# A fused encoder layer: tile 0's own queries among the attention pieces of tiles 1 to 3, paired forgetting scores, a fifth late query head

## The reference, cut to what matters

```
xn = rmsnorm(x); qa,ka,va,fa,qb,kb,vb = split(xn @ w_in)
A: 8 heads of 64: softmax(qa ka^T/8 + c_q - c_k, causal) va,   c = cumsum(log_sigmoid(fa + b_f))
B: 4 heads of 128: (softmax(q1 k1^T/8 + alibi) - lam softmax(q2 k2^T/8 + alibi)) vb, block-causal, rmsnorm
h  = x + [A || B] @ w_out
hn = rmsnorm(h); q = hn @ w_q                       # 8 retrieval heads, two halves of 128
s1,i1 = top16(q1 keys1^T); s2,i2 = top16(q2 keys2^T)
top16 of s1+s2 -> 16 experts e of 16384, gate g = softmax
h += sum_k gelu(u[e_k] . hn) g_k v[e_k];            out = rmsnorm_final(h)
```

## Time and profile before

| | us |
|---|---|
| median of the runs | 1546.19 |
| profiled execution, its own time | 1543.74 |
| its span, first to last instruction | 1542.0 |
| TensorE busy | 1278.2 (83%) |
| VectorE busy | 1078.2 (70%) |
| GpSimd busy | 757.8 (49%) |
| ScalarE busy | 459.6 (30%) |
| DMA moved | 596.5 MB, mean 387 GB/s |

### The profile page before, as it was taken

The page is one execution under the profiler, slowest core; times in us unless marked ns, Lnnn a source line. Parts: engine busy times, 40 slices in busy tenths (PEclk is TensorE's granted clock), DMA queues, the critical chain, the costliest instruction groups (busy, mean ns, idle before and its releaser), DMA issues.

```text
span 1542.0 us, 13063 instructions
## 1 busy us (share of the span) xinstructions
PE 1278.2 (83%) x3727; PEld 661.2 (43%) x3727; DVE 1078.2 (70%) x2520; ACT 459.6 (30%) x1200; POOL 757.8 (49%) x637
## 2 busy tenths in 40 slices
PE   9999999988888298999776788777787788777777
PEld 8776655665545144444332333332333333333333
DVE  3257699999988776666666676666666776666654
ACT  3432355466233032222222222221222222222212
POOL 0027477775677444454544544444455454444550
PEclk9999999998989599999999998899999999998999
DMA  9669799997999999999999999999999999999995
GB/s 381 260 248 414 277 324 347 374 376 262 350 362 392 400 391 407 423 421 421 422 421 422 421 422 421 421 422 421 421 421 422 422 421 422 422 421 421 421 421 215
DMA packets 99741, 596.50 MB, mean 387 GB/s; under 512 B 11480, under 2 KB 11480, under 8 KB 42328
## 3 DMA queue, kind: packets, MB, share of 16 engines
q0 software_dynamic: 89856, 536.91, 86.1%
q1 hardware_dynamic: 9816, 58.77, 9.5%
HBM read 593.54 MB, written 2.10 MB: 386 GB/s over the span
## 4 chain that ended last, share of the span: by engine, by line
DMA 43%; PE 15%; DVE 6%; POOL 2%; ACT 2%; issue 2%; DVEq 0%; POOLq 0%
PE acc L993 13%; DMA map_mem<-in_peer_uv_dram,eidx 9%; DMA w_ring<-in_peer_uv_dram,eidx 7%; DMA v_all<-in_peer_uv_dram,eidx 7%; DMA act_mem<-in_peer_uv_dram,eidx 6%; DMA mix_mem<-in_peer_uv_dram,eidx 5%; DMA v_ring<-in_peer_uv_dram,eidx 4%; DMA u_ring<-in_peer_uv_dram,eidx 4%; DMA v_ring<-in_peer_v_dram,eidx 2%; PE mm L785 1%; ACT diag L1226 1%; DVE map_mem L1544 1%; DVE w_ring L1544 1%; PE sc L785 1%; POOL v_ring L691 1%
## 5 line engine op out<-in xcount | busy, mean ns | idle before, releaser
L1219 ACT ACTIVATE gel<-hid 128x4 f32<-128x4 f32 x126 | 25.8, 205 | 713.7 <-DVE hid L1544 704.6
L684 POOL DMA_INDIRECT u_ring<-in_peer_u_dram,eidx x112 | 139.7, 1247 | 171.5 <-DVE eidx L1524 98.6
L993 PE MATMUL acc<-v_all,diag 128*128 128x512 f32 x256 | 128.3, 647 | 65.5 <-ACT diag L1226 65.0
L691 POOL DMA_INDIRECT v_ring<-in_peer_v_dram,eidx x112 | 132.3, 1182 | 64.0 <-DVE h L1572 35.4
L1572 DVE SCALAR_TENSOR_TENSOR h<-v_ring,coef,h 128x1024 f32<-128x1024 f32 x112 | 143.9, 1285 | 16.2 <-DMA v_ring<-in_peer_v_dram,eidx 13.0
L1536 DVE CUSTOM_DVE_ANT_0 u_ring<-u_ring,hn 128x1024 f32<-128x1024 f32 x112 | 136.4, 1218 | 14.0 <-DMA u_ring<-in_peer_u_dram,eidx 13.8
L993 PE MATMUL acc<-v_ring,diag 128*128 128x512 f32 x248 | 123.6, 645 | 27.2 <-ACT diag L1226 23.6
L993 PE MATMUL acc<-u_ring,diag 128*128 128x512 f32 x248 | 123.5, 645 | 26.1 <-ACT diag L1226 24.5
L993 PE MATMUL acc<-map_mem,diag 128*128 128x512 f32 x248 | 120.7, 633 | 25.3 <-ACT diag L1226 25.3
L1226 ACT ACTIVATE diag<-ident,coef 128x128 f32<-128x128 f32 x392 | 126.2, 390 | 48.2 <-DVE coef L1562 39.6
L710 POOL DMA_INDIRECT v_all<-in_peer_uv_dram,eidx x64 | 81.0, 1265 | 89.3 <-PE acc L993 81.4
(11 more groups left out here) (281 smaller groups left out, 2335.9 us busy)
## 6 DMA issues: line engine op xcount, KB each, us to landing
w_ring<-in_slabs_dram SPq DMA_DIRECT2D x29, 1024.0 KB, 8.3
v_ring<-in_slabs_dram SPq DMA_DIRECT2D x6, 1024.0 KB, 11.0
u_ring<-in_slabs_dram SPq DMA_DIRECT2D x6, 1024.0 KB, 11.4
map_mem<-in_slabs_dram SPq DMA_DIRECT2D x6, 1024.0 KB, 8.5
h<-in_x_dram SPq DMA_DIRECT2D x4, 512.0 KB, 13.1
u_ring<-in_peer_u_dram,eidx POOLq DMA_INDIRECT x112, 6.6
v_ring<-in_peer_v_dram,eidx POOLq DMA_INDIRECT x112, 6.9
v_all<-in_x_cols_dram SPq DMA_DIRECT2D x3, 512.0 KB, 7.3
```

Source lines behind the costliest of these rows:

```text
L684: nc.gpsimd.indirect_dma_start(out=u_ring[:, c % U_RING, :], out_offset=None, in_=peer_u[0], in_offset=bass.IndirectOffsetOnAxis(ap=eidx[n ...
L691: nc.gpsimd.indirect_dma_start(out=v_ring[:, c % V_RING, :], out_offset=None, in_=peer_v[0], in_offset=bass.IndirectOffsetOnAxis(ap=eidx[n ...
L993: last = nc.tensor.matmul(acc[half][:, :], diag[:, c % COLS, :], v_row(n, c)[:, half * BANK:(half + 1) * BANK], start=first, stop=(n % PH ...
L1219: nc.scalar.activation(gel[:, par, g0:g0 + COLS], hid[:, par, g0:g0 + COLS], ACT.Gelu).then_inc(gelu_done, 1)
```

## The change

It has four parts.

1. Order. Tile 0's remaining queries and keys (heads 3 to 7) no longer stand ahead of tiles 1 to 3, but among their pieces, head by head. For this tile 0's `hT` is kept in the memory of `gfb` (`h0T`), its query rows in a buffer of their own (`own_q`), and SP loads `gfb` after all slabs but the last two, once tile 0's last query is done.
2. The gates of tiles 1 to 3. "forget" (TensorE's product) comes before the last query/key slab of mixer A; "gate" (VectorE up to the absolute value, ScalarE's Exp and Ln) and "decay" (VectorE's cumulative sum) are pieces of their own. They cost 6 and 0 in the plan.
3. Scores of mixer A are made in pairs of heads at even steps: both products on 64 rows, then both on 40.
4. Five late heads instead of four. And ScalarE's GELU comes at gap 0 instead of gap 4.

```
-LATE_HEADS = 4
+LATE_HEADS = 5
+        gates = [("forget", g)] if g == 0 else [("gate", g), ("decay", g)]
+        ps += fox_in[:values_at] + gates + fox_in[values_at:values_at + 1] + [("selq", g, tiles[0])] + fox_in[values_at + 1:]
+        if g > 0:
+            ps.insert(ps.index(("project", g, 3, 0)), ("forget", g))
...
-    BEFORE, later = first_pieces[:cut_at], first_pieces[cut_at:] + pieces_of(1)
+    BEFORE, own, later = first_pieces[:cut_at], first_pieces[cut_at:], []
+    total, at = sum(share(p) for p in own + pieces_of(1)), 0.0
+    heads = [[p for p in own if p[0] == "query" and p[2] // 2 == hd] + [("keys", 0, hd)] for hd in range(EARLY_HEADS, PH)]
+    due = [(GRP * (i + 1) - 2) / (SLOTS - 1) for i in range(len(heads))]
+    for p in pieces_of(1):
+        if heads and not heads[0]:
+            heads.pop(0)
+            due.pop(0)
+        if heads and at / total >= due[0]:
+            later.append(heads[0].pop(0))
+            at += share(later[-1])
+        later.append(p)
+        at += share(p)
...
+        h0T = gfb[:, :].rearrange("p (c n) -> p c n", c=KC)
+        own_q = sb("own_q", [P, SLAB])
...
-            sp.dma_start(gfb[:, :], final_g.rearrange("(a n) -> a n", a=1).broadcast_to([P, D])).then_inc(out_done, 16)
             for n in range(N_IN + N_OUT + 2, len(slab_order) - 2):
                 load_slab(n)
+            sp.wait_ge(mm_full, mm_done(("query", 0, 2 * PH - 2)))
+            sp.dma_start(gfb[:, :], final_g.rearrange("(a n) -> a n", a=1).broadcast_to([P, D])).then_inc(out_done, 16)
...
+            def pair_scores(g, step):
+                t, first = at_step(g, 0, step)
+                nk, j = P * (t + 1), GROUPS[g].index(t)
+                if first == 0:
+                    pe.wait_ge(selq_ready, 2 * (t + 1))
+                both = [(HD * (m % 2), m // 2, map_no[(t, m)]) for m in (first, first + 1)]
+                for lo, ch, k in both:
+                    if k >= len(sc_b):
+                        pe.wait_ge(sc_drained, k + 1 - len(sc_b))
+                    nc.tensor.matmul(sc_b[k % len(sc_b)][:, 0:nk], qT[lo:lo + HD, ch, j * P:(j + 1) * P], kv_t[lo:lo + HD, ch, 0:nk],
+                                     start=True, stop=False)
+                for lo, ch, k in both:
+                    nc.tensor.matmul(sc_b[k % len(sc_b)][:, 0:nk], selq[lo:lo + 40, ch, t % 2, :], caug[lo:lo + 40, 0:nk],
+                                     start=False, stop=True).then_inc(sc_full, 1)
...
-                        if gap == COLS and (n or grp):
+                        if gap == 0 and (n or grp):
                             gelu(*group_at(GRP * n + grp - 1))
```

More of the change, by code:

```diff
@@ L183, in share @@
             return SHARE_ROWS[0] if by_rows else SHARE_COLS[0] + SHARE_COLS[1] * tiles
-        return {"norm1": 4, "xT": 2, "forget": 6, "mix": 4, "mixT": 1, "turn": 1, "selq": 2, "norm2": 4, "hT": 2, "lambda": 1, "lamrow": 1, "squares": 0, "factors": 0, "keys": 1.0 * tiles}[kind]
+        if kind == "forget":
+            return 6 if p[1] == 0 else 0
+        return {"norm1": 4, "xT": 2, "gate": 6, "decay": 0, "mix": 4, "mixT": 1, "turn": 1, "selq": 2, "norm2": 4, "hT": 2, "lambda": 1, "lamrow": 1, "squares": 0, "factors": 0, "keys": 1.0 * tiles}[kind]
     def woven(a, b):
@@ L265, in build @@
     cut_at = first_pieces.index(("keys", 0, EARLY_HEADS - 1)) + 1
-    BEFORE, later = first_pieces[:cut_at], first_pieces[cut_at:] + pieces_of(1)
+    BEFORE, own, later = first_pieces[:cut_at], first_pieces[cut_at:], []
[11 more added lines that the diff above has]
+        at += share(p)
+    assert not any(heads)
     AFTER = [[] for _ in range(SLOTS * GAPS)]
@@ L776, in rows_out @@
                             pe.wait_ge(first_slab, 16)
-                    last = nc.tensor.matmul(bk[:, 0:SLAB], (qT if name[0] == "query" else actT)[:, c, j * P:(j + 1) * P], w[:, c, :],
+                    last = nc.tensor.matmul(bk[:, 0:SLAB], (h0T if name[0] == "query" else actT)[:, c, j * P:(j + 1) * P], w[:, c, :],
                                             start=(c == 0), stop=(c == KC - 1))
@@ L796, in first_query @@
                         for c in range(4 * hf, 4 * hf + 4):
[L797 removed]
+                            last = nc.tensor.matmul(bks[c2][:, 0:P], w[:, c, c2 * P:(c2 + 1) * P], h0T[:, c, 0:P],
                                                     start=(c == 0), stop=(c == KC - 1))
@@ L800, in first_query, with turn @@
                             last.then_inc(mm_full, 1)
-            def turn(name, at):
+            def turn(name, src):
                 bk = mm_bank(name)
                 for q in range(2):
-                    last = nc.tensor.transpose(bk[:, q * P:(q + 1) * P], staged[:, at, q * P:(q + 1) * P], ident[:, :])
+                    last = nc.tensor.transpose(bk[:, q * P:(q + 1) * P], src[:, q * P:(q + 1) * P], ident[:, :])
                 last.then_inc(mm_full, 1)
@@ L822, in piece @@
                     pe.wait_ge(*emptied(("project", g, sl, 0)))
-                    turn((kind, *p), sl % 2)
+                    turn((kind, *p), staged[:, sl % 2, :])
                 elif kind == "forget":
@@ L882, in piece @@
                         pe.wait_ge(*emptied(("query", g, c2 - 1)))
-                        turn((kind, *p), c2 // 2 % 2)
+                        turn((kind, *p), own_q[:, :])
                 elif kind == "keys":
@@ L911, in attend @@
                 values(g, half, step)
+            def pair_scores(g, step):
[12 more added lines that the diff above has]
+                                     start=False, stop=True).then_inc(sc_full, 1)
             def scores(g, half, step):
-                if at_step(g, half, step):
+                if half == 0:
+                    if step % 2 == 0 and at_step(g, half, step):
+                        pair_scores(g, step)
+                elif at_step(g, half, step):
                     t, it = at_step(g, half, step)
                     nk, j = P * (t + 1), GROUPS[g].index(t)
-                    if it == 0:
-                        pe.wait_ge(selq_ready, 2 * (t + 1))
                     for m in maps_of(it):
@@ L1159, in piece @@
                     nc.scalar.activation(lam_s[0:1, 2:4], lam_s[0:1, 0:2], ACT.Exp).then_inc(act_norm, 1)
-                elif kind == "forget":
+                elif kind == "gate" or kind == "forget" and p[0] == 0:
                     n = P * len(GROUPS[p[0]])
@@ L1343, in piece @@
                                                 None, ALU.mult).then_inc(factors_ready, 1)
-                elif kind == "forget":
+                elif kind == "gate" or kind == "forget" and p[0] == 0:
                     g, = p
-                    n, t0 = P * len(GROUPS[g]), P * GROUPS[g][0]
+                    n = P * len(GROUPS[g])
                     dve.wait_ge(consts_in, 16 * 7)
@@ L1354, in piece @@
                     dve.wait_ge(*emptied(("forget", g) if g else ("fturn", 0)))
-                    from_act(nc.vector.scalar_tensor_tensor(out=e_f[:, 0:n], in0=z_f[:, 0:n], scalar=-1.0, in1=z_f[:, 0:n],
-                                                            op0=ALU.mult, op1=ALU.max), 2)
+                    nc.vector.scalar_tensor_tensor(out=e_f[:, 0:n], in0=z_f[:, 0:n], scalar=-1.0, in1=z_f[:, 0:n],
+                                                   op0=ALU.mult, op1=ALU.max).then_inc(norm_ask, 1)
+                    rooted[0] += 2
+                    if g == 0:
+                        piece("decay", 0)
+                elif kind == "decay":
+                    g, = p
+                    n, t0 = P * len(GROUPS[g]), P * GROUPS[g][0]
+                    dve.wait_ge(act_norm, rooted[0])
                     link(nc.vector.scalar_tensor_tensor(out=z_f[:, 0:n], in0=z_f[:, 0:n], scalar=0.0, in1=e_f[:, 0:n],
```

19 lines of the change are left out of this document (5 added, 14 removed).

## The result

The changed kernel takes 1552.86 us (median of 6 runs, 1552.02 to 1557.48), the kernel before 1545.97 in the same session: ratio 1.006 (95% interval 1.005 to 1.0069). The ratio is an estimate over all runs and not the quotient of the two medians, which is 1.0045. Its profiled execution took 1557.48 us (span 1555.6) against 1543.74; it lies 4.6 above its own median, so the traces overstate the difference (13.7 us for 6.9). A second profiled execution took 1554.2.

A forecast was written before the change was run, and what follows sets the result against it. VectorE's pace was taken to bound groups 2.0 to 5.3, bytes the end; the first groups could be won. 8.7 + 2.5 + 3.5 - 1.0 - 1.5 - 1.25 = 10.95 us off 1546.19 gave 1535.2 us, range 1525 to 1548.

The forecast's parts named there:

- groups 1.0 (rest) to 1.3: Groups 1.1 to 1.3: VectorE idles 3.6 us, mostly for scores; 2.5 us of it won, bounds 0 and 3.6.
- late stage: gain waited for and its bytes: Late stage: waiting for the final gain costs 1.5 us, its bytes moved into a full time another 1.25.
- What bounds the kernel: VectorE's own pace bounds groups 2.0 to 5.3, bytes the end after 610 us; groups 0.0 to 1.3 can be won.
- The gates and the order: Groups 0.3 to 1.0: gate numbers ready at 160.5 us instead of 175.99; 8.9 us won, 8.7 kept.
- the 1.2 us for tile 0's own pairs: Ahead of stage one: pairing tile 0's forgetting scores starts the projections 1.2 us earlier, at 105.3 us; bounds 0 and 2.5.
- The pairs: Eleven more score pairs save TensorE at most 21 us, counted as nothing on the path because VectorE hides them.
- The GELU: Group 6.0: GELU at gap 0 removes a 4.7 us stall; 3.5 us won, bounds 0 and 4.7.
- Two places: Two-place ring: TensorE stalls 16.4 us for slabs, mostly covered; cost 1.0 us, bounds 0 and 5.
- The final gain: First late output tile: the gain queued behind a slab stalls VectorE 2 to 7 us; cost 1.5, bounds 0 and 7.
- a stall of 0.5 us: Alternative for the final gain: at half rate each, slab and gain take 7.5 us, making the time 1.5 us lower.
- D: Rival, slower: TensorE sets the late stage's pace, the fifth late head costs 12 us; 1551 us, chance 0.16.
- C: Rival, no change: moved pieces meet a full VectorE and gains return as slab and row waits; 1546 us, chance 0.14.

The follow-up runs named there:

- free_place: The changed kernel, with each slab of the two-place ring put in the place whose last use is earlier, instead of strictly in turn: 1546.4 us, ratio 1.0008.
- mended: The changed kernel with slabs to the place freed first, the final gain loaded early and four late heads: 1544.7 us, ratio 0.9994.
- mended5: The changed kernel with slabs to the place freed first and the final gain loaded early, five late heads kept: 1544.2 us, ratio 0.9999.
- order_alone: Only the change's reordering, against the kernel before: ring in turn, gain early, single scores, GELU at gap 4, gates whole, four late heads; 1555.8 us, ratio 1.0077.
- gelu_gap4: The changed kernel with ScalarE's GELU back at gap 4 instead of gap 0: 1557.6 us, ratio 1.0085.
- before_five: The kernel before with five late heads, the remaining pieces spread anew by the plan: 1552.1 us, ratio 1.0054.

## Why the prediction was wrong, by its own steps

The ledger of the two profiled executions, in the order of the sum (positive is gained):

| step | forecast | measured |
|---|---|---|
| gates and order, to head 1's last dot of group 1.0 | 8.9 | 7.4 |
| groups 1.0 (rest) to 1.3 | 2.3 | -2.3 |
| groups 2.0 to 3.3 | 0 | -2.9 |
| groups 4.0 to 5.3, two-place ring | -1.0 | -13 |
| GELU at gap 0, 6.0 to the first late row | 3.5 | 4.4 |
| late stage: gain waited for and its bytes | -2.75 | -6.9 |
| behind it | 0 | -0.4 |
| sum | 10.95 | -13.7 |

The rows are named by the terms of the forecast; what stands in a row is not all that term's. In groups 4.0 to 5.3 free_place, where TensorE waits for no slab, still takes 123.0 us, against 127.8 in the changed kernel (124.5 in its second trace) and 114.8 before. So at most 5 of the 13 us went with the ring's waits, and 8 remain with the pieces where five late heads put them. mended, with four, takes 117.3 us there, but 110.8 in groups 2.0 to 3.3, where mended5 takes 106.2: the plan moves the time from one place to the other.

- **What bounds the kernel.** The step that failed first, and carried the 11.2 us of the order with it: "the second stretch is VectorE's own pace". VectorE's 7.4 us of idle in 220 was read rightly, but the row was too long. Its first half has TensorE busy 101.11 us of 105.5, its second 94.19 of 114.8; the average of 89% hid both. Two engines were full together there, and the new order puts two own heads of 4.4 us each into just this half. order_alone shows the price: it reaches group 2.0 at 226.2 us (before 228.4) and group 4.0 at 341.9 (before 333.9), and by the medians it ends 10.6 us slower, where the order was to win 8. In the full change the pairs take that load off, and VectorE's waits in this half are for rows (7.5 us, before 1.2), not for TensorE. What the changed kernel gained up to 2.0 (5.1 us) did not survive to 3.0 (0.5).
- **The gates and the order.** The working was right to 1.5 us, though the 1.2 us for tile 0's own pairs did not show (TensorE starts at 107.0). What it left out: the early lead is filled at once by the attention steps that stand earlier (from 1.0 gap 6 on), so VectorE's time goes to pieces, and in 1.1 to 1.3 the idle time rose from 3.5 to 4.2 us instead of falling by 2.5. VectorE's idle over the first eight groups fell from 31.7 to 25.0, not to 20.
- **The pairs.** "Nothing on the path" was wrong both ways: in the changed kernel they are worth 5.8 us, alone they are a loss. TensorE's saved time partly went back as lower clock: with pairs alone it stands idle for 52 us of stage one instead of 40, and is at 1.2 GHz for 66 us instead of 48. The Trainium skill, "TensorEngine Tiling (Array Packing)", section "Performance Considerations", has emptying PSUM as what tiling can't speed up. The trace agrees that the drains did not change: a score of 512 columns takes VectorE 0.68 us in both kernels. That was not what decided.
- **The GELU.** By the medians the size fits; the cause does not in the changed kernel: there the stall is gone at gap 4 too. The ledger's 4.4 us agree by luck: gelu_gap4 takes 51.9 us for the same stretch, the changed kernel 51.7.
- **Two places.** The mis-sized term: 1.0, bounds 0 to 5, measured 6.5 by the run with free places. I had 8.0 us for a slab; two that went out together took 10.3, and the product behind the wait, at the lower clock, 3.2 more. The waits for rows in 2.0 to 3.3 were not in the sum; free_place takes 4.8 us off this stretch. That they come of slabs loaded two at a time is argued, not shown. Ahead of the output addition TensorE waited for slabs three times, 1.9, 4.6 and 3.7 us where 0.8, 2.7 and 4.9 were forecast, and VectorE waited for TensorE only 1.2 us in groups 2.0 to 3.3: these were covered, as forecast.
- **The final gain.** The mechanism was right: 8.3 us of wait, above my 2 to 7, of which 2.6 (by the ratios 3.7) reached the end, where I had 1.5 with bounds 0 and 7. Slab and gain together took 13.3 us, near my upper bound of 14.5. The Trainium skill, "DMA: Bandwidth & Descriptors", section "Queues, rings and completion order", has the engines go round-robin between queue rows, packet by packet. That this gives each row half the bytes, and with it a stall of 0.5 us, was my own step; the 13.3 us speak against that step, and not against the rule.
- **Rivals.** D named the right side and 1551 of 1552.9, but with the wrong weights: of its 18.3 us the fifth head was 12 and measured 1 to 2.6. On the kernel before, the fifth head's cost came in stage one, by the stretched plan (405.0 us in before_five, before 397.1), which no part of the prediction had; with ring and gain mended it was gone. C came nearest in mechanism: pieces among the attention meeting a full engine is what order_alone shows, with TensorE as that engine, and slab and row waits are what the changed kernel shows. At no change its size was too mild.

Open: whether the mended order is worth more than the old one, what the GELU's gap does in the changed kernel, why pairs alone make the kernel before slower, and how much of the 13 us in groups 4.0 to 5.3 is whose.

## What to carry to other kernels

Before moving work into a stretch, split it until each part has one character: an engine that is the bound in one half and slack in the other looks covered on average. When work leaves a stage whose rest is spread by a plan, ask where the rest moves to. A ring "in turn" is only right while uses end in the order of loads; when the order changes, choose the place whose last use ends first, and keep loads of shared buffers off the queue position behind a slab.

## What the runs showed that was not expected

- Work taken off TensorE was not all time saved: with pairs alone its time at 1.2 GHz in stage one rose from 48 to 66 us, and the kernel became 0.2% slower.
- Less work in a stage made it longer: `LATE_HEADS = 5` alone lost 0.54%, with the same gaps it gained 0.1%.
- 512 KB issued 0.37 us behind a slab, while the queues moved 424 GB/s in all (568 to 575 us), took 13.3 us to land, the slab 9.8.
